# A two-block transformer kernel: rotary halves copied on ScalarE, retention values centred over each head as they leave PSUM, boundary norms split in two

## The chip, the cores and the metric

The kernel runs on one core of one Trainium2 chip. The time is that of one whole launch in microseconds (us) on the device. PE is TensorE, DVE is VectorE, ACT is ScalarE, POOL is GpSimd and SP is SyncE, which here issues every DMA.

## What is computed

Two blocks run one after the other on 256 tokens of width 1024, all in f32. The first block has two layers. A layer of it is:

```
h = rmsnorm(x, g_mix)
q_r, k_r, v_r, g_r, q_s, k_s, v_s, gate_a, gate_b = split(h @ w_in)
q_r, k_r = rotary(q_r), rotary(k_r) * 128 ** -0.5       # 4 heads of 128
ret = retention(q_r, k_r, v_r)                          # 4 heads, values of 256
ret = head_group_norm(ret) * silu(g_r)                  # (y - mean) * rsqrt(var + eps) over the 256
sb  = stick_breaking(q_s, k_s, v_s)                     # 8 heads of 128
merged = sigmoid(gate_a) * (ret @ p_ret) + sigmoid(gate_b) * (sb @ p_sb)
x = x + merged @ w_out
x = x + square(relu(rmsnorm(x, g_mlp) @ w_up)) @ w_down
```

`rotary(t)` is `[t1 * cos - t2 * sin, t1 * sin + t2 * cos]` over the two halves of a head's 128 columns. `head_group_norm` subtracts the mean of a head's 256 outputs and divides by their spread. For each token and head, retention is a weighted sum over earlier tokens of the value rows, so subtracting from every value row its own mean over the 256 columns of the head gives the same output as subtracting the mean afterwards. The second block is one layer with another mixer and the same kind of MLP, and a norm ends the whole.

## The kernel before, in words

The weights come as 201 pieces of 1 MB through a ring of four buffers (`raw`): the mixer of a layer of the first block has 44 pieces (k = 0 to 43), its MLP has 32; the second block has 17 and 32. PE works to nearly f32 precision with products of rounded parts: ACT rounds each piece to `w_hi` (L887), DVE subtracts to get `w_lo` (L1302, two instructions a piece), and PE multiplies hi by hi, hi by lo and lo by hi (all through `mm`, L488). `convert(piece)` stands for this step on either engine, and is called three pieces ahead of PE. Everything has a fixed order written out by hand on each engine, with semaphores between them; an engine that waits holds all that is behind it.

A use of a piece fills one of two pairs of PSUM banks. When PE is through with it, ACT copies one half (`carry`, L893), DVE adds the other (L1314) and frees the pair (`pair_free`), for which PE waits two uses later. Gate pieces (k = 20 to 31) have three more ACT and two more DVE instructions each.

The order of the mixer's pieces is: sbv 0 to 3, sbq/sbk 4 to 11, rq 12, 13, rk 14, 15, rv 16 to 19 (the retention values), rg 20 to 23, ga 24 to 27, gb 28 to 31, psb 32 to 35, pret 36 to 39, wout 40 to 43. `stages(k)` names small steps that each engine does at the end of piece k. Those that the change touches:

- `rotate` at k = 18 for q and at k = 19 for k. PE multiplies by the matrix `turn` (four records of 128x512), DVE multiplies the result by sin (L1464) into `ry`, POOL multiplies the original by cos (L1269), DVE adds (L1468). Then `rope_done` rises; PE waits for it at `ret_scores` of head 0, k = 21.
- `ret_out` of head h at k = 23 + 2h: PE makes the output, ACT copies it to `ry` (L980), POOL adds its halves to `rsum` (L1260).
- `ret_mean` at k = 25 + 2h: PE multiplies `rsum` by a matrix of 1/256, DVE subtracts this mean (L1475), ACT squares (L984), POOL adds (L1264, `rsq`).
- `ret_var` at k = 27 + 2h: PE takes the mean of `rsq`, ACT makes the reciprocal root (L988, L990), DVE multiplies by it (L1479), by the gate (L1482), and splits (L1484, L1308) to `retT`, which is needed at k = 36.
- Values: ACT copies one PSUM bank of rv (L1005), DVE the other (L1499), at k = 17 and 19.

Norms at the start of a layer, of the second block and at the end (`norm_rows`, `wide_rows`): ACT squares with a running sum (L899), POOL makes the factor (L1203, L1206), DVE makes `htok = xs * rstd * gain` in one instruction for each half of a tile (L1325, L1581; there are two tiles of 128 tokens). PE transposes `htok` (L520), ACT and DVE split it to `hT`. At the very start POOL raises `x_ready` for both tiles before it makes any factor, so it waits for the second tile of x. In an MLP the first use of a piece goes through `up`: DVE sums, squares, converts piece + 3 and only then rounds and splits `uT`, for which PE waits.

Of the kernel before, what the change touches and what calls it, by code (L numbers as in the profile page):

```python
# [21 lines left out]
F32 = mybir.dt.float32  # L22
# [4 lines left out]
ACT = mybir.ActivationFunctionType  # L27

# [53 lines left out]
def constants():  # L82
# [5 lines left out]
    rope = np.stack([np.cos(ang), np.sin(ang)], 1).astype(f)  # L88
# [11 lines left out]
    turn = np.zeros((P, P), f)  # L100
    turn[np.arange(half) + half, np.arange(half)] = -1.0
    turn[np.arange(half), np.arange(half) + half] = 1.0
    square = np.stack([np.eye(P, dtype=f), np.full((P, P), 1.0 / T, f), later, np.ones((P, P), f), turn], 1)
# [11 lines left out]
def build(nc, x, w_in, p_ret, p_sb, w_out, w_up, w_down, g_mix, g_mlp, g_final, norm_mix_g_2, w_in_2, pool_w_2,  # L115
# [3 lines left out]
    with ctx:  # L119
# [39 lines left out]
        sq_r = place("sq_r", [P, 5, P], F32R, at[0])  # L159
        sq_c = place("sq_c", [P, 5, P], F32)  # L160
        ident, mean_w, turn = (sq_c[:, i, :] for i in (0, 1, 4))
# [34 lines left out]
        rsum = place("rsum", [P, T], F32, htok_at)  # L196
# [4 lines left out]
        us = place("us", [P, 2, T], F32, y_at)  # L201
        usq = place("usq", [P, 2, T], F32, y_at + 2 * T * 4)
# [33 lines left out]
        def sem(name):  # L236
# [14 lines left out]
        x_ready = sem("x_ready")  # L251
# [18 lines left out]
        ret_scores, ret_decayed, ret_out, ret_copied, ret_mean, ret_centred, ret_squared, ret_var = (  # L270
            sem(n) for n in ("ret_scores", "ret_decayed", "ret_out", "ret_copied", "ret_mean", "ret_centred",
                             "ret_squared", "ret_var"))
# [53 lines left out]
        def stages(k):  # L326
# [49 lines left out]
        def _(sp):  # L376
# [42 lines left out]
            for L in range(DEPTH):  # L419
                for k in range(MIX_PIECES):  # L420
# [16 lines left out]
                    if k == 3 and L == 0:  # L437
                        sp.dma_start(sq_c[:, 1:5, :], square[:, 1:5]).then_inc(masks_in, 16)
                        sp.dma_start(mask_c[:, :], mask).then_inc(masks_in, 16)
# [38 lines left out]
            for t in range(TILES):  # L478

                sp.wait_ge(h_ready, 8 + 4 * 6 + 2 * (t + 1))  # L480
                sp.dma_start(ot[t], htok[:, t, :]).then_inc(out_sent, 16)
            sp.wait_ge(out_sent, 16 * TILES)
# [3 lines left out]
        def _(pe):  # L486
# [60 lines left out]
            def across_by_token(n, piece, use, between):  # L547
# [5 lines left out]
                hi_products(piece + 1, use + 1, 0)  # L553
                pe.wait_ge(h_lo, turned_at + 4)
# [20 lines left out]
            def mlp(n, stage, piece, use):  # L575

                turn_tile(n, 1, 0)
                across_by_token(n, piece, use, lambda: turn_tile(n, 1, 1))
# [53 lines left out]
            for L in range(DEPTH):  # L632
# [4 lines left out]
                def stage(name, i):  # L637
# [34 lines left out]
                    elif name == "rotate":  # L672

                        pe.wait_ge(pair_free, use_of("rk", 1, L).count(3))
                        pe.wait_ge(z_masked, Place(3, (L, 4)).count(1))
                        pe.wait_ge(consts_in, 32)
                        if i:
                            pe.wait_ge(rope_sin, Place(0, (L, 2)).count(1))
# [12 lines left out]

# [6 lines left out]
                    elif name == "ret_mean":  # L698
# [3 lines left out]
                        pe.wait_ge(ret_summed, head.count(0) * 2 + 1)  # L702
                        mm(ps[:, 6, 0:T], mean_w, rsum[:, :], True, True).then_inc(ret_mean, 1)
                    elif name == "ret_var":
                        pe.wait_ge(ret_summed, head.count(1) * 2)
                        mm(ps[:, 7, 0:T], mean_w, rsq[:, 0, :], True, True).then_inc(ret_var, 1)
# [68 lines left out]
            across_by_token(Place(4), Place(first), Place(use0), turn_other)  # L775
# [105 lines left out]
        def _(act):  # L881
# [13 lines left out]
            def square_sum(n, t, c):  # L895
# [3 lines left out]
                act.activation(htok[:, t, half], xs[:, t, half], ACT.Square, scale=D ** -0.5,  # L899
# [41 lines left out]
            for L in range(DEPTH):  # L941
# [3 lines left out]
                square_sum(mixer_norm, 0, 0)  # L945
                square_sum(mixer_norm, 0, 1)
                if not L:
                    convert(here)
                turned_hi(mixer_norm, 0, 0)
                turned_hi(mixer_norm, 0, 1)  # L950
                square_sum(mixer_norm, 1, 0)
                square_sum(mixer_norm, 1, 1)
# [6 lines left out]
                def stage(name, i):  # L959
# [12 lines left out]
                    elif name == "sb_out":  # L972
                        act.wait_ge(sb_out, pair.count(1))
                        act.activation(sbT[:, 2 * i:2 * i + 2, 0:T],
                                       ps[:, 6, :].rearrange("p (j t) -> p j t", j=2), ACT.Copy).then_inc(sb_hi, 1)
                    elif name == "ret_out":
                        act.wait_ge(ret_out, head.count(1))
                        if i >= 2:
                            act.wait_ge(ret_lo, head.count(-1))
                        act.activation(ry[:, i % 2, :, :], ps[:, 5, :].rearrange("p (e t) -> p e t", e=2),  # L980
                                       ACT.Copy).then_inc(ret_copied, 1)
                    elif name == "ret_mean":
                        act.wait_ge(ret_centred, head.count(1))
                        act.activation(rsq[:, :, :], ry[:, i % 2, :, :], ACT.Square).then_inc(ret_squared, 1)  # L984
# [881 lines left out]
```

## Time and profile before

| | us |
|---|---|
| median of 3 runs | 1282.72 |
| lowest, highest | 1282.07, 1284.2 |
| the profiled execution, whole | 1279.49 |
| its span, first to last instruction | 1277.7 |
| PE busy, of the span | 1233.7 |
| DVE busy | 872.8 |
| ACT busy | 629.5 |
| POOL busy | 55.0 |
| mean granted clock of TensorE | 0.999 |

The span is cut into what an engine did and what it waited for. A matmul's time in the trace overlaps with the next one's, so the cost of a matmul is read from the starts of the neighbours, not from its duration.

### The profile page before, as it was taken

Reading aid. Unit: us, or ns where it says so; the run is one execution under the profiler, and the core shown is the slowest. Engines: PE = TensorE matmul, PEld = TensorE weight load, DVE = VectorE, ACT = ScalarE, POOL = GpSimd, SP = SyncE. Lnnn points to the kernel's source line nnn. Section 1 sums busy time; section 2 is a strip of 40 time slices with the busy share of each in tenths; the row PEclk is TensorE's granted clock in tenths of the full one; section 3 lists DMA queues with packets and bytes.
Section 4 is the critical chain, followed back from the end, with each engine's and each line's share of the span. In section 5 each row is a group of like instructions: output and inputs, shape, how many; then the busy total and the mean of one; then the engine's idle time right before and its main releaser. Section 6 shows DMA issues by size and latency. Waiting matters only on the chain.

```text
span 1277.7 us, 17080 instructions
## 1 busy us (share of the span) xinstructions
PE 1233.7 (97%) x6842; PEld 1064.7 (83%) x6842; DVE 872.8 (68%) x1024; ACT 629.5 (49%) x827; POOL 55.0 (4%) x78
## 2 busy tenths in 40 slices
PE   4999999999999999999999999999989999999997
PEld 3888888788888887888888788888879997888886
DVE  4577767797566666667767887666677756766664
ACT  4455476644334434555576544443358456443442
POOL 0000110001000000000310001000010000100000
PEclk9999999999999999999999999999999999999999
DMA  5854455455555556655554555555656333555652
GB/s 199 273 159 160 138 165 159 158 176 187 171 197 182 183 194 199 191 148 161 152 162 151 164 174 188 193 179 186 213 165 190 100 100 132 185 182 192 197 181 98
DMA packets 162794, 219.92 MB, mean 172 GB/s; under 512 B 5680, under 2 KB 134064, under 8 KB 162736
## 3 DMA queue, kind: packets, MB, share of 16 engines
q1 hardware_dynamic: 162736, 219.11, 53.4%
q8 instruction: 41, 0.67, 0.2%
q14 instruction: 17, 0.14, 0.0%
HBM read 218.05 MB, written 1.05 MB: 171 GB/s over the span
## 4 chain that ended last, share of the span: by engine, by line
PE 83%; DVE 9%; ACT 4%; DMA 2%; issue 1%; POOL 0%; SPq 0%; DVEq 0%; POOLq 0%; ACTq 0%
PE ps L488 82%; DVE w_lo L1302 3%; DMA raw<-in_w_in_dram 1%; PE ps L520 1%; DMA xs<-in_x_dram 1%; ACT w_hi L887 1%; ACT carry L893 1%; DVE gates L1314 1%; ACT gates L1020 0%; DVE gtmp L1552 0%; DMA raw<-in_w_down_dram 0%; DVE gtmp L1547 0%; DVE ry L1479 0%; DVE ry L1482 0%; DVE retT L1308 0%
## 5 line engine op out<-in xcount | busy, mean ns | idle before, releaser
L488 PE MATMUL ps<-hT,w_hi 128*128 128x512 f32 (+1 forms) x1952 | 587.7, 367 | 1.6 <-DVE hT L1308 1.6
L1302 DVE TENSOR_TENSOR w_lo<-raw,w_hi 128x1024 fp32r<-128x1024 f32 x402 | 477.6, 1231 | 103.1 <-ACT w_hi L887 102.6
L887 ACT ACTIVATE w_hi<-raw 128x1024 fp32r<-128x1024 f32 x402 | 402.2, 1051 | 192.9 <-DMA raw<-in_w_up_dram 129.6
L488 PE MATMUL ps<-hT,w_lo 128*128 128x256 f32 x1696 | 455.3, 280 | 0.0
L488 PEld LDWEIGHTS ps<-hT,w_hi 128*128 128x128 f32 x1952 | 341.3, 189 | 64.1 <-DVE hT L1308 1.8
L488 PEld LDWEIGHTS ps<-hT,w_lo 128*128 128x128 f32 x1696 | 312.1, 189 | 2.4 <-issue 0.5
L488 PE MATMUL ps<-w_hi,uT 128*128 128x512 f32 x768 | 248.9, 396 | 5.0 <-DVE uT L1308 4.9
L893 ACT ACTIVATE carry<-ps 128x512 f32<-128x512 f32 x114 | 67.9, 595 | 254.8 <-PE ps L488 254.8
L488 PEld LDWEIGHTS ps<-w_hi,uT 128*128 128x128 f32 x768 | 144.3, 188 | 40.9 <-DVE uT L1308 6.4
L488 PE MATMUL ps<-w_lo,uT 128*128 128x512 f32 x384 | 151.8, 395 | 0.0
L488 PE MATMUL ps<-w_hi,hT 128*128 128x512 f32 (+1 forms) x480 | 143.5, 377 | 2.9 <-DVE hT L1308 1.5
L1374 DVE TENSOR_TENSOR us<-ps,carry 128x512 f32<-128x512 f32 x48 | 33.2, 691 | 116.2 <-ACT carry L893 116.1
L488 PEld LDWEIGHTS ps<-w_hi,hT 128*128 128x128 f32 x480 | 88.4, 190 | 19.6 <-issue 4.2
L488 PE MATMUL ps<-w_lo,hT 128*128 128x512 f32 (+1 forms) x240 | 89.1, 371 | 0.0
L488 PEld LDWEIGHTS ps<-w_lo,uT 128*128 128x128 f32 x384 | 72.2, 188 | 15.3
L488 PEld LDWEIGHTS ps<-w_lo,hT 128*128 128x128 f32 x240 | 45.7, 190 | 7.7 <-issue 0.5
L488 PE MATMUL ps<-sbT,w_hi 128*128 128x512 f32 x128 | 45.9, 400 | 0.0
L488 PE MATMUL ps<-retT,w_hi 128*128 128x512 f32 x128 | 45.3, 396 | 0.0
L488 PE MATMUL ps<-sbT,w_lo 128*128 128x256 f32 x128 | 36.1, 282 | 0.0
L488 PE MATMUL ps<-retT,w_lo 128*128 128x256 f32 x128 | 36.1, 282 | 0.0
L1378 DVE SCALAR_TENSOR_TENSOR usq<-us 128x512 f32<-128x512 f32 x48 | 33.3, 693 | 1.6
L1308 DVE TENSOR_TENSOR uT<-usq,uT 128x512 fp32r<-128x512 f32 x48 | 33.2, 693 | 1.6
(188 smaller groups left out, 946.9 us busy)
## 6 DMA issues: line engine op xcount, KB each, us to landing
raw<-in_w_in_dram SPq DMA_DIRECT2D x77, 1024.0 KB, 5.7
raw<-in_w_up_dram SPq DMA_DIRECT2D x48, 1024.0 KB, 5.4
raw<-in_w_down_dram SPq DMA_DIRECT2D x48, 1024.0 KB, 4.9
raw<-in_w_out_dram SPq DMA_DIRECT2D x12, 1024.0 KB, 5.1
raw<-in_p_sb_dram SPq DMA_DIRECT2D x8, 1024.0 KB, 5.1
raw<-in_p_ret_dram SPq DMA_DIRECT2D x8, 1024.0 KB, 5.0
xs<-in_x_dram SPq DMA_DIRECT2D x2, 512.0 KB, 6.9
gain<-in_g_mix_dram SPq DMA_DIRECT2D x2, 512.0 KB, 6.8
```

The lines of the kernel that those rows point to most:

```text
L488: return pe.matmul(o, lhsT, rhs, start=start, stop=stop)
L520: last = pe.transpose(ps[:, token_bank(t, c), k * P:(k + 1) * P], htok[:, t, c * HALF + k * P:c * HALF + (k + 1) * P], ident)
L887: act.activation(w_hi[:, s, half], raw[:, s, half], ACT.Copy).then_inc(hi_ready, 1)
L893: act.activation(carry[:, use.slot(2), :, :], ps[:, b:b + 2, T:2 * T], ACT.Copy).then_inc(pair_act, 1)
L1302: last = dve.tensor_tensor(w_lo[:, s, half], raw[:, s, half], w_hi[:, s, half].bitcast(F32), ALU.subtract)
L1308: return dve.tensor_tensor(o, value, hi.bitcast(F32), ALU.subtract)
L1314: dve.tensor_tensor(o, ps[:, b:b + 2, 0:T], carry[:, use.slot(2), :, :], ALU.add).then_inc(pair_free, 1)
L1374: dve.tensor_tensor(us[:, :, :], ps[:, b:b + 2, 0:T], carry[:, use.slot(2), :, :], ALU.add).then_inc(pair_free, 1)
L1378: dve.scalar_tensor_tensor(out=usq[:, :, :], in0=us[:, :, :], scalar=0.0, in1=us[:, :, :], op0=ALU.max, op1=ALU.mult).then_inc(u_squared, 1)
```

## The change

- Rotary: ACT copies the two halves of the partitions crosswise from `retqkv` into `ry` (two instructions of 64 partitions x 1024); the sign is in the sin table. DVE multiplies `ry` by sin in place, in SBUF. The matrix `turn` and its products are gone.
- Retention values: ACT copies nothing. DVE sums each head's 256 columns in PSUM (one reduction over both banks) and writes both banks centred (two instructions). `ret_mean`, `rsum`, the subtraction and ACT's copy of the outputs are gone. ACT squares the outputs straight from PSUM; DVE multiplies them by the gate as they leave PSUM; `ret_var` comes two pieces earlier (k = 25 + 2h). PE's `ret_out` of a head now waits until ACT and DVE have read the one before.
- Norms: DVE multiplies by the gain (`gained`) before the factor is there, and a `tensor_scalar` in place after it. The squares go to `junk` and not to `htok`.
- Start: POOL raises `x_ready` for tile 0, makes its factor, and then waits for tile 1. ACT and DVE split tile 0 before they convert piece 0.
- MLP: the first `up` rounds and splits before DVE converts piece + 3.
- Second block: PE does the first products of piece 1 before it transposes tile 1.
- End: the result leaves in four DMAs of half a tile instead of two of a tile.

```diff
                     elif name == "rotate":
-                        for j in range(2):
-                            last = mm(ps[:, 4 + j, :], turn, retqkv[:, 2 * j:2 * j + 2, i, :], True, True)
-                        last.then_inc(turned, 1)
+                        act.wait_ge(pair_free, use_of("rk", 1, L).count(3))
+                        act.wait_ge(rest_split, Place(3, (L, SB_H // 2)).count(1))
+                        if i:
+                            act.wait_ge(rope_done, Place(0, (L, 2)).count(1))
+                        swapped = ry[:, :, :, :].rearrange("p a e t -> p (a e) t")
+                        act.activation(swapped[0:P // 2], retqkv[P // 2:P, :, i, :], ACT.Copy)
+                        act.activation(swapped[P // 2:P], retqkv[0:P // 2, :, i, :], ACT.Copy).then_inc(turned, 1)
...
-                        dve.tensor_tensor(tmp, ps[:, 4:6, :].rearrange("p b (h t) -> p (b h) t", h=2),
-                                          rope_c[:, 1:2, :].to_broadcast([P, RET_H, T]), ALU.mult).then_inc(rope_sin, 1)
+                        dve.tensor_tensor(tmp, tmp, rope_c[:, 1:2, :].to_broadcast([P, RET_H, T]), ALU.mult).then_inc(rope_sin, 1)
...
-                                dve.tensor_copy(retqkv[:, 2 * (i // 2):2 * (i // 2) + 2, 3, :],
-                                                b.rearrange("p (h c) -> p h c", h=2)).then_inc(pair_free, 1)
+                                b = ps[:, bank:bank + 2, :].rearrange("p t (h c) -> p t h c", h=2)
+                                sums = v_sums[:, :].rearrange("p (t h) -> p t h", t=TILES)
+                                dve.tensor_reduce(sums, b, X_AXIS, ALU.add).then_inc(v_summed, 1)
+                                dve.wait_ge(v_summed, Place(i // 2, (L, 2)).count(1))
+                                for t in range(TILES):
+                                    last = dve.scalar_tensor_tensor(
+                                        out=retqkv[:, 2 * (i // 2):2 * (i // 2) + 2, 2 + t, :],
+                                        in0=sums[:, t, :].unsqueeze(2).to_broadcast([P, 2, T]), scalar=-1.0 / T,
+                                        in1=b[:, t], op0=ALU.mult, op1=ALU.add)
+                                last.then_inc(pair_free, 1)
...
-                        act.activation(ry[:, i % 2, :, :], ps[:, 5, :].rearrange("p (e t) -> p e t", e=2),
-                                       ACT.Copy).then_inc(ret_copied, 1)
-                    elif name == "ret_mean":
-                        act.wait_ge(ret_centred, head.count(1))
-                        act.activation(rsq[:, :, :], ry[:, i % 2, :, :], ACT.Square).then_inc(ret_squared, 1)
+                        act.activation(rsq[:, :, :], ps[:, 5, :].rearrange("p (e t) -> p e t", e=2),
+                                       ACT.Square).then_inc(ret_squared, 1)
...
                     elif name == "ret_out":
                         pe.wait_ge(ret_decayed, head.count(1))
+                        pe.wait_ge(ret_gated, head.count(0))
+                        pe.wait_ge(ret_squared, head.count(0))
...
-            for name, at_piece in (("ret_var", 27), ("ret_mean", 25), ("ret_out", 23), ("ret_scores", 21)):
+            for name, at_piece in (("ret_var", 25), ("ret_out", 23), ("ret_scores", 21)):
...
-                    dve.scalar_tensor_tensor(out=htok[:, t, q], in0=xs[:, t, q], scalar=rstd[:, t:t + 1],
-                                             in1=gain[:, n.slot(2), q], op0=ALU.mult, op1=ALU.mult).then_inc(h_ready, 1)
+                    dve.wait_ge(row_gained, m.count(0) * 4 + (2 * t + c + 1))
+                    dve.tensor_scalar(htok[:, t, q], htok[:, t, q], rstd[:, t:t + 1], None, ALU.mult).then_inc(h_ready, 1)
...
-                up(piece, use, count(0), 0, before=False)
+                up(piece, use, count(0), 0, before=False, ahead=False)
+                convert(piece + 3)
...
-            across_by_token(Place(4), Place(first), Place(use0), turn_other)
+            across_by_token(Place(4), Place(first), Place(use0), lambda: None, turn_other)
```

## Rows read from the trace of the kernel before

**Rows 1.** The page, part 1: busy time, share, count

```profile
PE 1233.7 (97%) x6842; PEld 1064.7 (83%) x6842; DVE 872.8 (68%) x1024; ACT 629.5 (49%) x827; POOL 55.0 (4%) x78
```

**Rows 2.** Waits of PE: waiting, releaser, total us, times, longest

```profile
...
PE ps L488 <- POOL rsq L1264: 5.2, 2, 2.6
PE ps L488 <- DVE uT L1308: 4.9, 3, 1.6
...
PE ps L520 <- DVE htok L1581: 2.0, 1, 2.0
```

**Rows 3.** Timeline of PE, first layer: start, length, what

```profile
143.03 1.93 PE L488 MATMUL ps<-retqkv,sq_c 128*128 128x512 f32 x4
...
144.40 0.79 PE L488 MATMUL ps<-w_hi,hT 128*128 128x512 f32 x1
...
145.03 0.39 PE L488 MATMUL ps<-w_lo,hT 128*128 128x512 f32 x1
...
189.32 0.59 PE L488 MATMUL ps<-rsum,sq_c 128*128 128x256 f32 x2
...
189.75 1.47 PE L488 MATMUL ps<-rs,retqkv 128*128 128x256 f32 x8
```

**Rows 4.** Timeline ahead of the variance product of head 3, first layer

```profile
243.14 0.68 DVE L1475 TENSOR_TENSOR ry<-ry,ps 128x512 f32<-128x512 f32 x1
243.86 0.63 ACT L984 ACTIVATE rsq<-ry 128x512 f32<-128x512 f32 x1 [3.27 <-DVE ry L1475]
...
244.56 0.73 POOL L1264 TENSOR_TENSOR rsq<-rsq 128x256 f32<-128x256 f32 x1 [14.15 <-ACT rsq L984]
```

**Rows 5.** Timeline of DVE at the start of the first MLP

```profile
313.38 2.35 DVE L1302 TENSOR_TENSOR w_lo<-raw,w_hi 128x1024 fp32r<-128x1024 f32 x2
...
316.11 0.69 DVE L1308 TENSOR_TENSOR uT<-usq,uT 128x512 fp32r<-128x512 f32 x1
```

**Rows 6.** The start: one DMA with its landing, then the timeline

```profile
gain<-in_g_mix_dram SPq DMA_DIRECT2D x1, 512.0 KB, 5.4
...
1.48 0.34 SPq L387 DMA_DIRECT2D gain<-in_g_mix_dram  x1
...
4.42 0.63 ACT L899 ACTIVATE htok<-xs 128x512 f32<-128x512 f32 x1 [2.40 <-POOLq L1231]
...
11.73 2.00 ACT L887 ACTIVATE w_hi<-raw 128x1024 fp32r<-128x1024 f32 x2 [5.98 <-DMA raw<-in_w_in_dram]
...
14.25 1.42 DVE L1325 SCALAR_TENSOR_TENSOR htok<-xs,rstd,gain 128x512 f32<-128x512 f32 x2 [14.25 <-POOL rstd L1206]
...
18.64 0.77 PE L488 MATMUL ps<-w_hi,hT 128*128 128x512 f32 x1 [1.55 <-DVE hT L1308]
```

**Rows 7.** Timeline around the rotary steps, first layer

```profile
145.04 2.42 POOL L1269 TENSOR_TENSOR retqkv<-retqkv,rope_c 128x1024 f32<-128x1024 f32 x1 [125.05 <-PE ps L488]
...
145.13 0.85 ACT L971 ACTIVATE wts<-logw 128x768 f32<-128x768 f32 x1 [2.35 <-DVE logw L1452]
...
152.06 4.57 DVE L1302 TENSOR_TENSOR w_lo<-raw,w_hi 128x1024 fp32r<-128x1024 f32 x2 [0.25 <-ACT w_hi L887]
...
152.25 3.30 POOL L1269 TENSOR_TENSOR retqkv<-retqkv,rope_c 128x1024 f32<-128x1024 f32 x1 [4.79 <-PE ps L488]
...
164.51 0.70 PE L488 MATMUL ps<-retqkv 128*128 128x256 f32 x3
```

**Rows 8.** Groups by line: shapes, count, busy us, mean ns, idle before

```profile
L887 ACT ACTIVATE w_hi<-raw 128x1024 fp32r<-128x1024 f32 x402 | 402.2, 1051 | 192.9 <-DMA raw<-in_w_up_dram 129.6 <-DMA raw<-in_w_in_dram 41.0 <-DMA raw<-in_w_down_dram 16.5
...
L1547 DVE TENSOR_SCALAR gtmp<-gates 128x512 f32<-128x512 f32 x16 | 6.8, 427 | 0.5
...
L1468 DVE TENSOR_TENSOR retqkv<-retqkv,ry 128x1024 f32<-128x1024 f32 x4 | 4.9, 1226 | 2.5 <-POOL retqkv L1269 2.3
L1464 DVE TENSOR_TENSOR ry<-ps,rope_c 128x1024 f32<-128x1024 f32 x4 | 4.9, 1214 | 0.0
```

**Rows 9.** Timeline at the end

```profile
1273.25 1.41 DVE L1325 SCALAR_TENSOR_TENSOR htok<-xs,rstd,gain 128x512 f32<-128x512 f32 x2 [1.83 <-POOL rstd L1206]
```

More of the change, by code:

```diff
@@ L87, in constants @@
     ang = np.arange(T, dtype=f)[None, :] * np.concatenate([inv_freq, inv_freq])[:, None]
-    rope = np.stack([np.cos(ang), np.sin(ang)], 1).astype(f)
+    turned_sign = np.where(np.arange(P) < half, f(-1.0), f(1.0))[:, None]
+    rope = np.stack([np.cos(ang), np.sin(ang) * turned_sign], 1).astype(f)
     s, t = np.arange(P)[:, None], np.arange(P)[None, :]
@@ L99, in constants @@
     later = (s > t).astype(f)
[L100 to L103, printed above, removed]
+    square = np.stack([np.eye(P, dtype=f), np.full((P, P), 1.0 / T, f), later, np.ones((P, P), f)], 1)
     levels = np.zeros((P, MASKED, CHUNK), f)
@@ L158, in build @@
         gn_eps = place("gn_eps", [P, 1], F32)
-        sq_r = place("sq_r", [P, 5, P], F32R, at[0])
-        sq_c = place("sq_c", [P, 5, P], F32)
-        ident, mean_w, turn = (sq_c[:, i, :] for i in (0, 1, 4))
+        v_sums = place("v_sums", [P, 2 * TILES], F32)
+        sq_r = place("sq_r", [P, 4, P], F32R, at[0])
+        sq_c = place("sq_c", [P, 4, P], F32)
+        ident, mean_w = (sq_c[:, i, :] for i in (0, 1))
         later, ones = sq_r[:, 2, :], sq_r[:, 3, :]
@@ L478, in _ @@
             for t in range(TILES):
-                sp.wait_ge(h_ready, 8 + 4 * 6 + 2 * (t + 1))
-                sp.dma_start(ot[t], htok[:, t, :]).then_inc(out_sent, 16)
-            sp.wait_ge(out_sent, 16 * TILES)
+                for c in range(2):
+                    half = slice(c * HALF, (c + 1) * HALF)
+                    sp.wait_ge(h_ready, 8 + 4 * 6 + 2 * t + c + 1)
+                    sp.dma_start(ot[t][:, half], htok[:, t, half]).then_inc(out_sent, 16)
+            sp.wait_ge(out_sent, 16 * 2 * TILES)
         @block.tensor
@@ L545, in lo_products, with across_by_token @@
                 last.then_inc(piece_used, 1)
-            def across_by_token(n, piece, use, between):
+            def across_by_token(n, piece, use, between, after):
                 turned_at = n.count(0) * 4
@@ L553, in across_by_token @@
                 hi_products(piece + 1, use + 1, 0)
+                after()
                 pe.wait_ge(h_lo, turned_at + 4)
@@ L697, in stage @@
                         last.then_inc(ret_out, 1)
-                    elif name == "ret_mean":
+                    elif name == "ret_var":
                         if i == 0:
                             pe.wait_ge(sb_lo, Place(3, (L, 4)).count(1))
[L702 to L705, printed above, removed]
+                        pe.wait_ge(ret_summed, head.count(1))
                         mm(ps[:, 7, 0:T], mean_w, rsq[:, 0, :], True, True).then_inc(ret_var, 1)
@@ L1405, in _, with row @@
                 before = (Place(1), Place(1), Place(0), Place(MIX_PIECES))
+                def row(t, c):
+                    if L:
+                        down_sum(*before, t, c)
+                    gained(mixer_norm, mixer_norm, Place(L), t, c)
+                row(0, 0)
+                row(0, 1)
                 if L:
-                    down_sum(*before, 0, 0)
-                    down_sum(*before, 0, 1)
                     convert(here + 1)
-                norm_rows(mixer_norm, Place(L), 0)
+                norm_rows(Place(L), 0)
                 if L:
-                    down_sum(*before, 1, 0)
-                else:
-                    convert(here)
+                    row(1, 0)
                 turned_lo(mixer_norm, 0, 0)
                 turned_lo(mixer_norm, 0, 1)
-                if L:
-                    down_sum(*before, 1, 1)
-                norm_rows(mixer_norm, Place(L), 1)
+                if not L:
+                    convert(here)
+                    row(1, 0)
+                row(1, 1)
+                norm_rows(Place(L), 1)
                 if not L:
```

125 lines of the change are left out of this document (62 added, 63 removed).

## The prediction

> **What bounds the kernel now.** I read the page's busy times first. PE is busy 1233.7 us of a span of 1277.7, 97% [rows 1]; DVE, next, has 68%. So work taken from PE counts in full, idle time of PE counts in full, and time of DVE, ACT or POOL counts only where PE ends up waiting for it. The second view is what PE waited for. Three entries of it are places that the change touches: 5.2 us in two waits for POOL's `rsq`, 4.9 us in three waits for `uT`, and 2.0 us for `htok` at the second block's start [rows 2]. The wait before the first transpose is the start of the program and is read from its timeline. Third, I read the timeline of each place, since a step's worth is that of the wait that ends last there. The granted clock is at full rate over nearly all of the span, so no stretch but the start is priced at the half rate.
>
> **Rotary products.** Four `rotate` steps (two a layer) leave PE. One starts at 143.03, the next ordinary product at 144.40, and that product's record is 0.79 long where its neighbour's is 0.39 [rows 3]: 1.37 + 0.40 = 1.77 us each, so 4 x 1.77 = 7.1 us off PE.
>
> **Mean products.** From the start of the `rsum` product to the next one are 189.75 - 189.32 = 0.43 us [rows 3]. Eight of them: 3.4 us.
>
> **The wait for the variance.** In each layer PE stands 2.6 us before the last `ret_var`. What comes late is a chain through DVE's subtraction, ACT's square and POOL's sum, 243.14 to 245.3 [rows 4], and DVE reaches that subtraction late since it runs behind PE through the gate pieces. After the change the square reads PSUM directly, at ACT's step of k = 29, with no DVE instruction ahead of it in the chain, and PE asks for the sum at the end of k = 31. PE's 1233.7 us over 201 pieces are 6.1 us each with the small steps, some 5.6 without; by two gate pieces of that length there are about 4 us of room. I take the wait as gone: 2 x 2.6 = 5.2 us. Bounds 0 and 5.2: if DVE lags so far that ACT's gate steps slip, part stays.
>
> **The MLP's first product.** PE waits 1.6 us, three times, for `uT` [rows 2]. Ahead of its rounding DVE does a conversion of 2.35 us [rows 5]. With this moved behind, `uT` comes 2.3 us earlier, which is more than 1.6: 4.9 us gained. What is late next is the moved conversion itself. It would end about 1.2 us later than now, but PE first does a down product of some 5.6 us, so it is covered; were that cover gone, it would cost 1.2 each.
>
> **The start.** Now the first product starts at 18.64 [rows 6]. The chain to it goes through the factor, which POOL makes only when the second tile of x is in; the rows of `htok` start at 14.25. After the change, tile 0 is squared from 4.42, the factor is there at about 6.8, and the gain lands at 1.48 + 5.4 = 6.9. Two gain multiplications (0.69 each), two scalings (0.43) and the transposes and splits end by 12.3. Then the weights are last: ACT rounds piece 0 from 11.73 to 13.73 and DVE's two conversions follow it half by half, to 15.15. So the first product starts near 15.2: 3.4 us earlier. Piece 1 must be ready 4.7 us on; its rounding waits for its landing and DVE's conversion comes after the gain and the rows of tile 1. I get 19.8 against a need of 19.9, where before PE stood 0.4: 3.9 us in all. Products at this point run at half the later pace, as their starts show; if the clock rises not with the products but at the same instant as now, up to 1.7 us of the gain is lost. Bounds 2 and 4.5.
>
> **Second block's start.** PE now idles 2.0 us for tile 1's `htok` [rows 2] with 1.9 us of products still in hand. The change does these first, but then PE stands until ACT and DVE have split tile 1, about 2 us after the transpose. The rows of tile 1 themselves come 0.3 us sooner, through the shorter instruction. Net 0.9 us; bounds 0 and 2.0.
>
> **The end.** After the last factor DVE needs 1.41 us [rows 9]; with two `tensor_scalar` at 0.43 [rows 8] it needs 0.86, 0.55 less. The last DMA carries half, and starts while the first half is on its way: some 0.6 less. 1.2 us; bounds 0.5 and 1.6. The 0.43 is measured with a constant, and the new instruction takes its scalar per partition, which no row here shows for this operation. The Trainium skill (VectorE: DVE Perf Modes, The perf-mode tier table) puts f32 `tensor_scalar` from SBUF at twice the rate of `tensor_tensor`, with no exception for such a scalar; if it did not hold, the end would gain about 0.6 and not 1.2.
>
> Sum of gains: 7.1 + 3.4 + 5.2 + 4.9 + 3.9 + 0.9 + 1.2 = 26.6 us. At a layer's start in the second layer PE waits for the split, which doesn't move: nothing.
>
> **What the change adds: the rotary stretch.** This is where PE's products are replaced by work of engines that are less busy, but in a chain with a date: `rope_done` must be up when PE ends piece 21. I follow the first layer on its own time axis. ACT ends the weights' exponential at 145.13 + 0.85 = 145.98 [rows 7]; then come its two copies. No row shows 64 partitions from one half to the other; the nearest is 1.05 for 128x1024 [rows 8], which I take; below it could be nothing less than half, above it twice if crossing partitions costs. So `turned` is up at 148.1 (before: 145.0). Now DVE multiplies by sin, 1.23 from SBUF for the sum of the same shape [rows 8], and POOL by cos, 2.42 alone. Do they run side by side? Before, DVE read PSUM there, and lost nothing. But at 152.06, when DVE's two conversions with both inputs in SBUF fell on POOL's second cos, they took 4.57 and not 2.35, and POOL took 3.30 and not 2.42 [rows 5, 7]: DVE lost 2.2. So I put the two in series: 148.1 + 1.23 + 2.42, and DVE's sum of 1.23: 153.0. Then ACT copies for k, 155.1. DVE meanwhile does the values of k = 19: the reduction of 1024 elements from PSUM at 1.21 for the nearest row [rows 8], two centrings at 0.69: 155.8. POOL's second cos runs to 157.6 and holds DVE's conversion of piece 22, which ends at 160.0; sin 161.2; sum 162.5. PE ended piece 21 at 164.51 [rows 7]; less the two rotary steps of 3.5 it is there at 161.0. It stands 1.4 us. DVE then is behind PE by a piece and frees PSUM pairs late: about 0.7 us more until k = 24 (its step of a gate piece, 4.1 plus two turns of 0.6 with ACT, is just under PE's 5.6, so it hardly catches up, but falls no further). 2.1 us a layer, 4.2 in all. Bounds 0 (copies of half the length) and 10 (copies of double length, 4.2 more on the chain).
>
> The Trainium skill (SBUF — State Buffer, Who interferes with whom) calls this an exclusive lock: a DVE instruction with two SBUF inputs and a GpSimd one that reads SBUF exclude each other for a whole instruction. The rows agree: 3.30 is 2.42 and most of a conversion, 4.57 is 2.35 and most of the cos. It speaks against moving the sin product to SBUF; without such a lock the chain would be 1.2 us shorter.
>
> **What hides the rest.** The values at k = 17: 2.6 us on DVE for 0.69 before; DVE has idle time before its next conversion, and the pair is wanted two uses on. Gate multiplication moves from `ret_var` to `ret_out`: DVE now waits at k = 23 for ACT's square (0.6), but saves the subtraction (0.68) for each head. ACT no longer waits for `ret_lo` or the centring in the middle of its queue, which had held its next `carry`. PE's new waits at `ret_out` (`ret_gated` of the head before, a DVE step of two pieces earlier): by the same count DVE is through 2 to 4 us before PE asks. These go at 0, bounds -1 and 2 us in all.
>
> **Sum.** 26.6 - 4.2 = 22.4 us. The span goes from 1277.7 to 1255.3, the profiled execution from 1279.49 to 1257.1. The median of the runs lies 3.2 us above that execution, so the forecast is 1282.72 - 22.4 = 1260.3.
>
> **Rivals.**
> *The rotary stretch is covered.* ACT copies of half the partitions are cheap, or DVE's order absorbs them. For it: DVE is busy 68% of the span, and its idle time lies in just such places. Then 1282.7 - 26.6 = 1256.1. Chance 0.22.
> *DVE's lag spreads.* For it: DVE runs only a few tenths per piece faster than PE through the gates, so a lag of a piece lasts; against: it is never two pieces. With 5 us a layer: 1282.7 - 26.6 + 10 = 1266.1. Chance 0.15.
> *Slower than before.* The crosswise copy is the one unmeasured operation on a dated chain. It stands four times, two instructions each. If `rope_done` came over 13.3 us after PE wants it in each layer (copies of 4 us or so each instead of 1.05), the gain would be used up; at 5 us each the four copies of a layer add 4 x 3.95 = 15.8 to the chain, 2 x (15.8 + 2.1) - 26.6 = 9.2 lost: 1291.9. Against: every ACT copy in the trace goes by elements per partition. Chance 0.03.
> *The boundaries don't give what they say.* The conversion moved behind `uT`, the early factor and the split rows only shift which wait is last; half of 4.9 + 3.9 + 0.9 + 1.2 stays: 1265.8. Chance 0.07.
> The forecast as worked out has 0.53.
>
> **Numbers.** Range 1254.5 to 1267. A measurement of this kernel tells about 0.2% (2.6 us) from no change. Faster by more: 0.96; within: 0.01; slower: 0.03.
>
> **What would show it.** PE's busy time down by about 10 us, no records of `turn` or `rsum`; no wait for `rsq`, none for `uT`; the first product near 15.2; a new wait of PE for `retqkv` (L1468's sum) of 1 to 1.5 us, twice; crosswise copies near 1.05 us. The forecast is wrong if the copies take twice that, if PE shows waits for `pair_free` through the gate pieces, or if the first product starts after 17.

## The result

The changed kernel takes 1264.74 us (median of 4 runs, 1264.06 to 1265.52) against 1282.39 for the kernel before in the same series: a ratio of 0.9874, 95% interval 0.9859 to 0.989. The forecast was 1260.3, with a range of 1254.5 to 1267. The sign and most of the gain were right, and the time lies in the range, 4.4 us above the forecast. One run of the kernel with the old addresses (below) took 3145 us and is left out; the median of its other five is 1261.33, where the expectations have 1261.84. The profiled execution of after took 1264.06 us with a span of 1262.2, where before it was 1279.49 and 1277.7. The busy line and PE's waits in the profile of after (waiting, releaser, total us, times, longest):

```profile
PE 1230.4 (97%) x6810; PEld 1062.0 (84%) x6810; DVE 882.0 (70%) x1040; ACT 630.2 (50%) x823; POOL 53.3 (4%) x70
```

```profile
PE ps L489 <- DVE w_lo L1292: 4.6, 2, 4.1
PE ps L489 <- DVE hT L1298: 3.1, 2, 1.6
...
PE ps L489 <- DVE retqkv L1469: 2.1, 2, 1.1
PE ps L489 <- DVE gtmp L1304: 1.4, 2, 1.1
...
PE ps L521 <- DVE htok L1596: 0.6, 1, 0.6
```

Against [rows 2] the waits for `rsq` and for `uT` are gone, `htok` fell from 2.0 to 0.6, and the new wait for `retqkv` (the rotary sum, L1469) is there, twice. All of that was forecast. Two things don't fit. L1304 is the sum with which DVE frees a PSUM pair; PE waits for it at k = 34 of both layers, 0.3 and 1.1 us. The forecast had pairs freed late only up to k = 24, at 0.7 us a layer. And PE's busy time fell by 3.3 us against [rows 1], where the products taken out are worth 10.5. So PE does the work that is left more slowly, and no wait shows this.

The start, in the timeline of after:

```profile
7.31 0.87 DVE L1322 TENSOR_SCALAR htok<-htok,rstd 128x512 f32<-128x512 f32 x2
...
10.40 1.99 ACT L877 ACTIVATE w_hi<-raw 128x1024 fp32r<-128x1024 f32 x2
...
11.48 2.36 DVE L1292 TENSOR_TENSOR w_lo<-raw,w_hi 128x1024 fp32r<-128x1024 f32 x2 [0.25 <-ACT w_hi L877]
...
13.99 0.76 PE L489 MATMUL ps<-w_hi,hT 128*128 128x512 f32 x1 [4.12 <-DVE w_lo L1292]
```

The rows of the first tile are made at 7.31 where [rows 6] have 14.25, and then the weights are last, as forecast. The first product starts at 13.99, not 15.2: piece 0 could be rounded at 10.40, where [rows 6] have 11.73.

The rotary stretch of the first layer in after:

```profile
141.53 1.06 ACT L975 ACTIVATE ry<-retqkv 64x1024 f32<-64x1024 f32 x1
...
142.60 1.06 ACT L976 ACTIVATE ry<-retqkv 64x1024 f32<-64x1024 f32 x1
...
143.69 1.23 DVE L1466 TENSOR_TENSOR ry<-ry,rope_c 128x1024 f32<-128x1024 f32 x1 [3.06 <-ACT ry L976]
143.73 3.47 POOL L1259 TENSOR_TENSOR retqkv<-retqkv,rope_c 128x1024 f32<-128x1024 f32 x1 [128.27 <-ACT ry L976]
...
147.24 1.23 DVE L1469 TENSOR_TENSOR retqkv<-retqkv,ry 128x1024 f32<-128x1024 f32 x1 [2.32 <-POOL retqkv L1259]
...
150.78 2.45 POOL L1259 TENSOR_TENSOR retqkv<-retqkv,rope_c 128x1024 f32<-128x1024 f32 x1 [3.58 <-ACT ry L976]
150.83 4.61 DVE L1292 TENSOR_TENSOR w_lo<-raw,w_hi 128x1024 fp32r<-128x1024 f32 x2
...
156.68 1.23 DVE L1469 TENSOR_TENSOR retqkv<-retqkv,ry 128x1024 f32<-128x1024 f32 x1
...
157.96 0.92 PE L489 MATMUL ps<-retqkv 128*128 128x256 f32 x4 [1.01 <-DVE retqkv L1469]
```

The copies take 1.06 each (forecast 1.05). POOL's product, 2.42 alone [rows 7], takes 3.47 beside DVE's sine product of 1.23, which is near the sum of the two, 3.65. DVE's conversion takes 4.61 beside the other, which is close to 2.35 + 2.45. PE then waits 1.01, forecast 1.4.

### The profile page after: what moved, and what is told of

It is laid out like the page before. It is cut to its first block, busy times and chain, and to the rows that moved or that the text cites. A ratio compares the mean times of both kernels' runs of the same rounds, so it can differ in the third digit from the quotient of the medians.

```text
span 1262.2 us, 17060 instructions
## 1 busy us (share of the span) xinstructions
PE 1230.4 (97%) x6810; PEld 1062.0 (84%) x6810; DVE 882.0 (70%) x1040; ACT 630.2 (50%) x823; POOL 53.3 (4%) x70
## 3 DMA queue, kind: packets, MB, share of 16 engines
HBM read 217.98 MB, written 1.05 MB: 174 GB/s over the span
## 4 chain that ended last, share of the span: by engine, by line
PE 59%; issue 19%; DVE 13%; ACT 5%; DMA 2%; POOL 2%; DVEq 0%; SPq 0%; POOLq 0%; ACTq 0%
PE ps L489 59%; DVE w_lo L1292 5%; DVE gtmp L1561 1%; DMA raw<-in_w_in_dram 1%; DVE gates L1304 1%; DVE gtmp L1556 1%; ACT gates L1015 1%; DMA decay_c<-in_decay_dram 1%; ACT w_hi L877 1%; PE ps L521 1%; POOL retqkv L1259 1%; POOL gr L1246 1%; DVE retT L1484 0%; ACT junk L891 0%; DVE ry L1482 0%
```

## Experiments

Times below are medians beside runs of the kernel before on the same chip (1280.86, 1280.84 and 1281.82 us in the three series). Where single stages are compared, I take the same instruction in two traces (ACT's `carry` number n) and look how far one kernel is ahead. The old-address kernel, the early copies and the conversion put back ran in different series; the kernel before differs by 1 us between these.

**The two kernels again.**

> The kernel before, unchanged, beside the changed kernel on one chip. In the two profiles, four pieces of an MLP took 22.31 us before and 22.46 us after, 0.7% more, though the loop is the same. Theory A, the pace belongs to the chip or the execution: here before and after show the same MLP pace, within 0.1%, and the span of before is near 1282 to 1284 if the pace is the slow one. Theory B, the change makes PE slower: before keeps 22.31 and after 22.46 side by side.

> The changed kernel, unchanged. Theory A: the same MLP pace as the kernel before on this chip, and 17 to 20 us less than it at that pace. Theory B: 22.46 us for four pieces against 22.31. In both, two stretches of half clock of 3.4 us, one at the second block's start and one at its wout products, if they belong to the kernel; at other places or missing if they are chance.

Before: 1280.22 us, a single run. After: 1264.68 (1263.25 to 1266.19), ratio 0.9883, 0.9867 to 0.99. The medians of the two series differ by 16.2 and 17.7 us. The paces are those of the first two traces, 22.31 and 22.47, so Theory B holds. Of the stretches at half clock the one at the second block's start came again, at 942.9; the other did not, and the kernel before had one of its own at 245.4.

**The order of the second block's start, undone.**

```diff
-            across_by_token(Place(4), Place(first), Place(use0), lambda: None, turn_other)
+            across_by_token(Place(4), Place(first), Place(use0), turn_other, lambda: None)
```

> Changed kernel with the second block's tile 1 transposed between the hi products of pieces 0 and 1 again, as before. Theory A, that the new order puts PE's idle time of the second block's start together (1.6, 0.6, 0.9 and 1.55 us within 10 us) and that the clock falls for it: the half clock there is gone and the kernel is 1 to 2 us faster than the changed one. Theory B, that the half clock comes by chance of position: it stays, and this order is 0 to 1 us slower.

1265.37 us, 0.9877 (0.9858 to 0.9897): no difference from after beyond the noise of some 2 us. PE's wait for `htok` is back (2.5 us against 0.6), and a wait for `hT` is gone (1.6 against 3.1). One wait is exchanged for the other: the term is worth nothing that can be measured. The half clock at the second block's start is gone, as Theory A said, but the trace has a stretch of 6.8 us at 974.1 instead, in a wait of 2.9 us for `hq`, so the time doesn't fall.

**PE's rotary products back in the changed kernel.** The matrix `turn`, its products and the sine product from PSUM are as before; the rest of the change stays.

> Changed kernel with the rotary products on PE again (the matrix, DVE's product from PSUM), all else as changed. The prediction's step: the swap takes 1.77 us off PE four times and gives 2.1 a layer back as waits, so this kernel is 2.9 us slower than the changed one, about 1267.5; its PE has no wait for retqkv L1469. The rival that the rotary stretch costs nothing: 7 us slower. That it costs more than it gives: faster than the changed one. Its tiles lie 32 bytes further than before, so its pace tells on the address theory too: A says 22.46, B leaves it open.

1265.62 us, 0.9881 (0.9859 to 0.9903): the same as after within the noise, and less than the 1267.5 expected. Its MLP pace is that of after, as theory A of the addresses said. PE has no wait for `retqkv`, and the four `turn` steps instead. By the traces the mixers of the two layers are 1.0 and 0.3 us slower than with the copies: the swap is worth 1.3 us, where the forecast had 7.1 - 4.2 = 2.9.

**The rotary steps two pieces earlier.**

```diff
-            if k in (18, 19):
-                todo.append(("rotate", k - 18))
+            if k in (16, 17):
+                todo.append(("rotate", k - 16))
...
-                        act.wait_ge(rest_split, Place(3, (L, SB_H // 2)).count(1))
```

> Changed kernel with the rotary steps two pieces earlier (k = 16 and 17), without the wait for rest_split. Theory A, that the rotary chain is late by 1 to 2 us a layer for PE: PE's waits for retqkv L1469 and the late pair_free go, 2 to 4.5 us faster than the changed kernel. Theory B, that DVE's total work in the stretch is what counts and not the date of the chain: the wait only moves to another line, 0 to 1 us.

1276.47 us, 0.9963 (0.9949 to 0.9977), 11.8 slower than after. Neither theory had this. Its waits of PE begin:

```profile
PE ps L489 <- DVE rest_lo L1297: 14.9, 3, 6.3
```

The steps now stand on ACT and DVE ahead of the last stick-breaking split, for which PE has a date too. The waits for `retqkv` and for the pair are gone. From inside the two waits of 6.3 us come stretches at half clock of 10.2 and 6.8 us, which are part of the loss. In the first layer a DVE instruction of 0.95 fell on POOL's product and took 3.09:

```profile
135.09 2.39 POOL L1258 TENSOR_TENSOR retqkv<-retqkv,rope_c 128x1024 f32<-128x1024 f32 x1 [117.99 <-ACT ry L975]
135.21 3.09 DVE L1447 SCALAR_TENSOR_TENSOR zs<-zs,soft 128x768 f32<-128x768 f32 x1
```

**PE's pace: addresses or instructions?** The rows below are ACT's `carry` behind one up-projection of the first MLP and behind the one 20 pieces on, where PE never waits: first before, then after. The rows of after stand one up-projection later in the MLP; the pace is even over both stretches.

```profile
328.31 0.60 ACT L893 ACTIVATE carry<-ps 128x512 f32<-128x512 f32 x1 [5.42 <-PE ps L488]
...
439.84 0.60 ACT L893 ACTIVATE carry<-ps 128x512 f32<-128x512 f32 x1 [3.52 <-PE ps L488]
```

```profile
327.28 0.60 ACT L883 ACTIVATE carry<-ps 128x512 f32<-128x512 f32 x1 [3.61 <-PE ps L489]
...
439.64 0.60 ACT L883 ACTIVATE carry<-ps 128x512 f32<-128x512 f32 x1 [3.69 <-PE ps L489]
```

Twenty pieces take 111.53 us before and 112.36 after, 0.7% more, with the same products at the full clock. The change takes out one matrix of 512 bytes per partition and puts in sums of 32 bytes, so the tiles behind them lie 480 bytes lower, an odd multiple of 32. The weights and `hT` lie ahead of them and did not move; `uT` did. Four kernels ask what makes the difference. The first gives the changed kernel the old addresses:

```diff
-        v_sums = place("v_sums", [P, 2 * TILES], F32)
...
+        v_sums = place("v_sums", [P, 2 * TILES], F32)
+        place("unused", [P, 120], F32)
```

> Changed kernel with every tile behind sq_c at its address in the kernel before (the change moved them by -480 bytes, an odd multiple of 32), by 480 unused bytes. Nothing else differs. Side by side on one chip the MLP went at 22.31 us for four pieces before and at 22.45 to 22.47 after. Theory A, the pace comes from where the tiles lie: 22.31 here, and a kernel 5 to 8 us faster than the changed one, 1257 to 1260. Theory B, it comes from the order and number of PE's instructions: 22.45 to 22.47 and 1264 to 1265 here.

1261.33 us, 0.9846 (0.9825 to 0.9866): by the medians 3.4 us faster than after, less than the 5 to 8 expected. In the profiles PE is busy 4.0 us less (1226.4 for 1230.4), with the same 6.8 us at half clock in each.

```profile
328.05 0.60 ACT L884 ACTIVATE carry<-ps 128x512 f32<-128x512 f32 x1 [3.49 <-PE ps L490]
...
439.58 0.60 ACT L884 ACTIVATE carry<-ps 128x512 f32<-128x512 f32 x1 [3.67 <-PE ps L490]
```

111.53 us, the pace of before, with the instructions of after. The second moves the tiles of the kernel before by 32 bytes (`place("unused", [P, 8], F32)` ahead of them):

> The kernel before with 32 unused bytes ahead of sq_r, so that all later tiles lie 32 bytes further. Theory A (addresses): the MLP pace goes from 22.31 to about 22.46 and the kernel is 4 to 8 us slower than before. Theory B (instructions): no change, within 1 us.

1288.21 us, 1.0058 (1.0037 to 1.0079), at the pace of after: 112.36. Not all of the 7.4 us is pace, since its trace has three stretches of 3.4 us at half clock where the first trace of before has none ahead of the end. The third only adds an instruction to PE's queue (`pe.wait_ge(small_set, 1)`, ahead of the layers):

> Changed kernel with one more instruction on PE, a wait for something long since there, ahead of the first layer. Theory B, that the place of PE's instructions in memory sets the pace: another pace than 22.45 to 22.47 in some of the MLPs. Theory A: the same pace.

1264.34 us, a single run, with the pace of after unchanged. With the first kernel, where the pace changed and the instructions did not, this leaves the place of PE's instructions without support as a cause. A fourth, in the kernel before, lowers one tile alone:

```diff
-        uT = place("uT", [P, 3, 2, 2 * T], F32R, u_at)
+        uT = place("uT", [P, 3, 2, 2 * T], F32R, u_at - 32)
```

> The kernel before, with one tile alone 32 bytes lower: the MLP's activation uT, which its down-projections stream. If the pace follows the address of the tile that streams, four pieces take between 22.31 and 22.46 us: the half of the products that stream uT are slow and those that stream hT keep their pace, so about 22.38, and 1.5 to 2 us on the whole. If it follows the address of the matrix that is loaded (the pieces' high and low parts, which do not move here), 22.31 and no difference. If any odd multiple of 32 does it to all, 22.46 and about 3.6 us.

1284.31 us, 1.0021 (1.0011 to 1.0032).

```profile
330.41 0.60 ACT L893 ACTIVATE carry<-ps 128x512 f32<-128x512 f32 x1 [5.55 <-PE ps L488]
...
442.44 0.60 ACT L893 ACTIVATE carry<-ps 128x512 f32<-128x512 f32 x1 [3.68 <-PE ps L488]
```

112.03 us: 0.50 of the 0.83. So one tile alone makes 60% of the loss; which other tile gives the rest was not tried. The expectation has two things wrong, though. In `mm(out, loaded, streamed)` a down-projection passes `uT` as the matrix that is loaded and streams the weights (`three`); `hT` is streamed by the up-projections (`across`), with the weights loaded. And the time is not lost where `uT` is read. In the trace's names the streamed tile stands first. Each series below is the first product of one up-projection, of the down-projection behind it, and of the next up-projection: before, then with `uT` moved.

```profile
322.56 0.39 PE L488 MATMUL ps<-hT,w_hi 128*128 128x512 f32 x1
...
328.11 0.39 PE L488 MATMUL ps<-w_hi,uT 128*128 128x512 f32 x1
...
333.71 0.39 PE L488 MATMUL ps<-hT,w_hi 128*128 128x512 f32 x1
```

```profile
324.56 0.39 PE L488 MATMUL ps<-hT,w_hi 128*128 128x512 f32 x1
...
330.21 0.40 PE L488 MATMUL ps<-w_hi,uT 128*128 128x512 f32 x1
...
335.82 0.40 PE L488 MATMUL ps<-hT,w_hi 128*128 128x512 f32 x1
```

The up-projection takes 5.55 and 5.65 us, the down-projection 5.60 and 5.61. From here on, with `uT` moved, every second up-projection takes 5.65 and the others 5.55. Over ten of each, the up-projections take 55.54 us before, 55.99 with `uT` moved and 56.20 in after; the down-projections 55.99, 56.05 and 56.17. So most of the loss lies in products that read neither `uT` nor any other tile that moved. The runs show that the layout sets the pace; they don't show by what way, and PE's own reads of the moved tile can't be all of it. Nor does a run show that odd multiples of 32 are what matters: every shift tried (480, 32 and 32 bytes the other way) was one, and no even multiple was tried.

**The MLP's first conversion back ahead of `uT`** (from here on with the old addresses, so beside 1261.33):

```diff
-                up(piece, use, count(0), 0, before=False, ahead=False)
-                convert(piece + 3)
+                up(piece, use, count(0), 0, before=False)
```

> The changed kernel with the tiles at the old addresses (1261.84 us), but the first up-projection converts piece + 3 ahead of the rounding of its own activation, as before the change. Theory of the prediction (the reorder is worth 1.6 us three times, 4.9 us; the trace after gave 1.9 three times): three waits for uT of 1.6 us are back and the time is 1266.5 to 1267.5 us. Rival (the conversion only moves, so the next products wait for it anyway): no more than 2 us slower, under 1264 us, with a wait for the converted piece gone in exchange.

1266.46 us, 0.9878 (0.9862 to 0.9893): 5.1 slower by the medians and 4.1 by the ratios, as the theory said, and the line is back:

```profile
PE ps L490 <- DVE uT L1299: 4.9, 3, 1.6
```

**Copies and cosine product one piece earlier, DVE's part where it was.**

```diff
+            if k in (17, 18):
+                todo.append(("turn_in", k - 17))
...
-                    elif name == "rotate":
+                    elif name == "turn_in":
 
                         act.wait_ge(pair_free, use_of("rk", 1, L).count(3))
-                        act.wait_ge(rest_split, Place(3, (L, SB_H // 2)).count(1))
...
-                        elif name == "rotate":
+                        elif name == "turn_in":
```

> The changed kernel with the tiles at the old addresses (1261.84 us), and of the rotary swap only ScalarE's two copies and GpSimd's cosine product go ahead by one piece, into the hole of ScalarE beside the last 2.3 us for the decay rows; VectorE's sine product and sum keep their place. Theory (the chain copy, product, sum sets a date that TensorE waits for): TensorE's two waits for the turned values (2.2 us in all) and half of the 2 us of late work behind them go, 1258 to 1260 us, and no row of waits names L1470. Rival (what costs is VectorE's work itself and the port that it shares with GpSimd): the conversion of 1.2 us that now lies beside the cosine product stretches as the other did (4.6 us), the first waits for decay or pieces return, and the time is 1261 to 1266 us. A copy of 1.06 us needs no longer while a piece is converted.

1255.93 us (1254.78 to 1257.63), 0.9794 (0.978 to 0.9807): 5.4 us faster by the medians than the same kernel without this edit, and 5.4 in the traces at the end of the second layer's MLP. It is the fastest kernel here that does all the work. The gain is larger than the 2 to 4 expected. No wait names the rotary sum. Its timeline:

```profile
135.41 1.06 ACT L977 ACTIVATE ry<-retqkv 64x1024 f32<-64x1024 f32 x1
...
136.48 1.06 ACT L978 ACTIVATE ry<-retqkv 64x1024 f32<-64x1024 f32 x1
...
137.62 2.84 POOL L1261 TENSOR_TENSOR retqkv<-retqkv,rope_c 128x1024 f32<-128x1024 f32 x1 [120.89 <-ACT ry L978]
...
138.66 4.01 DVE L1294 TENSOR_TENSOR w_lo<-raw,w_hi 128x1024 fp32r<-128x1024 f32 x2 [0.48 <-ACT w_hi L880]
...
154.18 1.23 DVE L1471 TENSOR_TENSOR retqkv<-retqkv,ry 128x1024 f32<-128x1024 f32 x1
...
157.86 0.82 PE L492 MATMUL ps<-retqkv 128*128 128x256 f32 x4
```

DVE's conversions are still stretched (4.01 here for 2.35), but the second sum ends 2.5 us before PE wants it. To see what that gives, take ACT's `carry` at k = 14 and k = 34 of the first layer, the latter in the `p_sb` product: before, old addresses, and this kernel.

```profile
114.65 0.60 ACT L893 ACTIVATE carry<-ps 128x512 f32<-128x512 f32 x1 [2.97 <-PE ps L488]
...
251.83 0.60 ACT L893 ACTIVATE carry<-ps 128x512 f32<-128x512 f32 x1 [1.78 <-PE ps L488]
```

```profile
110.80 0.60 ACT L884 ACTIVATE carry<-ps 128x512 f32<-128x512 f32 x1 [2.97 <-PE ps L490]
...
242.35 0.60 ACT L884 ACTIVATE carry<-ps 128x512 f32<-128x512 f32 x1 [3.55 <-PE ps L490]
```

```profile
111.29 0.60 ACT L886 ACTIVATE carry<-ps 128x512 f32<-128x512 f32 x1 [3.16 <-PE ps L492]
...
240.71 0.60 ACT L886 ACTIVATE carry<-ps 128x512 f32<-128x512 f32 x1 [3.09 <-PE ps L492]
```

137.18, 131.55 and 129.42 us. The forecast's gains for one layer, without any cost of the rotary stretch, are 2 x 1.77 + 4 x 0.43 + 2.6 = 7.9; the first and third differ by 7.76. In the second layer the three are 137.19, 132.34 and 129.31, so 7.88. The sum of the gains is thus confirmed, not each of them.

**Without POOL's cosine product.** Its two instructions a layer are left out, so the rotary values are not the reference's:

```diff
-                            pool.tensor_tensor(v, v, rope_c[:, 0:1, :].to_broadcast([P, RET_H, T]),
-                                               ALU.mult).then_inc(rope_cos, 1)
+                            pool.sem_inc(rope_cos, 1)
```

> The changed kernel with the tiles at the old addresses (1261.84 us), without GpSimd's cosine product (its two instructions per layer are left out, so the rotary values are wrong; nothing else is). It gives the price of what lies beside it: theory (the port is what makes VectorE late: its conversion took 4.6 us beside the product of 2.45 us and GpSimd's other product 3.5 us): that conversion takes 2.2 to 2.4 us, the sums come 2 to 3 us earlier, the waits for L1470 go, and the time is 1257.5 to 1260 us. Rival (VectorE has the slack, and copies and sums alone set the date): within 1 us of 1261.84.

1253.77 us, 0.9788 (0.9769 to 0.9807), faster than either side expected. DVE's conversion is at its length alone:

```profile
149.71 2.35 DVE L1292 TENSOR_TENSOR w_lo<-raw,w_hi 128x1024 fp32r<-128x1024 f32 x2
```

At the end of the second layer's MLP it is 5.9 us ahead of the same kernel with the product, and only 0.5 ahead of the kernel with early copies. So when the chain starts a piece earlier, the cosine product and what it stretches cost next to nothing. This kernel leaves out the product and the stretching together, so it doesn't part the two.

## Why the prediction was right, and where it missed

The mechanism held: the waits and products that it named are gone, and the rotary stretch costs PE something in each layer. That the time still lies in the range owes something to the width of the range, since two costs of some 3 us each were in no term.

Each term of the sum, measured between the kernel before and the changed kernel with the old addresses, which run at one pace:

- *Start*, 3.9 forecast: 4.0. Right: the first product starts at 15.09, 3.6 us earlier (forecast 3.4). In after it started at 13.99, since piece 0 could be rounded sooner there; over the traces with the new start it lies between 13.99 and 16.16, with the rounding of piece 0 between 10.40 and 12.57. The kernel before varies in the same way (17.63 to 19.05), so a pair of traces tells this term to 2 us or so.
- *Mixers of the two layers* (rotary and mean products, variance wait, less the rotary stretch), 15.7 - 4.2 = 11.5 forecast: 5.6 + 4.9 = 10.5. The early copies show the sum of the gains to be right, 7.76 and 7.88 of 7.9. The term that was mis-sized is the stretch: 2.2 and 3.0 us instead of 2.1 each. The working had the mechanism, down to the length of the conversion. PE's wait for the sum was 1.1 us in each layer and not 1.4; its waits for a free pair, forecast at 0.7 up to k = 24, were 0.2 and 0.9, nearly all at k = 34; the remaining 1 us a layer is in no large wait of the profile, and it goes with the wait when the copies come earlier. So the 0.7 for all that DVE's lag costs behind the sum was too little.
- *MLP's first product*, 4.9 forecast: 5.8 by the traces (1.9 three times), 4 to 5 by the runs with it undone. Right, within 1 us.
- *Second block's start*, 0.9 forecast: 0.3 lost by the traces, no difference by the run with it undone. PE stands 0.62 us for `htok` where it stood 1.96, but then 1.55 us for the split of that tile, during which, before, it had products to do. The step that failed is the balance of the two: the 1.9 us of products moved ahead do not shorten the way through transpose and split, and this way costs PE all that they hide.
- *End*, 1.2 forecast: about 0.8, within its bounds. The last factor's rows take less, as the rule on `tensor_scalar` had it (the Trainium skill, VectorE: DVE Perf Modes, The perf-mode tier table), also with a scalar per partition:

```profile
1258.62 0.88 DVE L1322 TENSOR_SCALAR htok<-htok,rstd 128x512 f32<-128x512 f32 x2 [1.10 <-POOL rstd L1204]
```

That is 0.88 where [rows 9] have 1.41.

Two things were in no term. The first is the addresses: 3.4 us by the medians, 3.6 by the traces. With the half clock (below), which adds some 3.2 us to PE's busy time in after, they account for a fall of 3.3 us instead of 10.5. I read "PE's busy time falls by 10 us" from records taken out, and took for granted that the records left keep their length. The diff shows two tile declarations changed; I passed over them.

The second is the clock. The forecast took full rate from the profile of before for every stretch but the start. The profile of after has two stretches of half rate (granted clock 0.5, 1.2 GHz), 3.4 us each, at 942.0 and 1051.2; the first began in a wait of PE of 1.6 us, the second 1.3 us behind one of 2.6. The columns are stretch, length, PE busy, granted clock, DMA share, GB/s:

```profile
1051.20:1054.60 3.40, 3.40 (x10) 0.50 0.15 57
1055.00:1058.00 3.00, 3.00 (x14) 1.00 0.00 0
```

The same sixteen products of the second block take 3.51 us in after and 2.18 with the old addresses, where they ran at full rate:

```profile
942.36 3.51 PE L489 MATMUL ps<-hT,w_hi 128*128 128x256 f32 x16 [1.55 <-DVE hT L1298]
```

```profile
940.96 2.18 PE L490 MATMUL ps<-hT,w_hi 128*128 128x256 f32 x16 [1.55 <-DVE hT L1299]
```

Both stood 1.55 us before, so the wait alone doesn't decide it. The kernel with the old addresses has its stretch at 971.1 instead, 6.8 us long, from inside a wait of 3.1 for `hq` that lasts 1.2 us more. The second execution of the kernel before has one of 3.4 at 245.4, behind the variance wait, where the first has none. A stretch of 3.4 us in which PE doesn't stand does 1.7 us less work.

The account for the kernel with the old addresses: 22.4 forecast, less 1.6 for the misses of the terms (+0.1, -1.0, +0.9, -1.2, -0.4), less 2.8 for the clock (half of the 5.6 us in which PE did not stand) is 18.0; the spans differ by 17.1. Of the 0.9 between, 0.5 lies in the second block behind its start, where PE waits 3.1 us for `hq` and before waited 1.7; the rest is not assigned. For after: 22.4 less 1.6, less some 3.6 for the addresses, less 3.2 for the clock is 14.0, and the spans differ by 15.5. Of the 1.5 between, 0.7 is the start of this execution. The rest fits the wait for `hq`, which is 1.3 us here instead of 3.1: PE comes there later for the half clock, and so part of that loss is taken back.

Of the rivals, the one with slow copies fell with the first row of 1.06. *The boundaries don't give what they say* had 1265.8, the nearest to the time, but not by its reason: of the 10.9 us of these terms 10.3 stayed in the traces. *DVE's lag spreads* had 1266.1: there is a wait for a free PSUM pair, but of 1.1 us at most, and the stretch cost 5.2 us in all and not 10. *The stretch is covered* describes what the kernel with early copies then does: 1255.93, where that rival said 1256.1. That the two agree so closely is partly chance, since this kernel too has the loss at the second block and one half-rate stretch, which that rival had not.

## What to carry to other kernels

When work moves from the full engine to engines with room, look at the date of the chain first: moving only its head by one piece, into an idle hole, with the busy engine's steps left in place, brought 5.4 us where the whole swap had brought 1.3; moving all of it by two pieces brought a loss of 11.8 us. No run moved all of it by one piece. After any change in what is allocated, compare the pace of a stretch without waits in both traces before explaining the sum; a product that is 0.7% slower shows in no wait. And check in the code which operand is loaded and which is streamed before building a test on it. Count short stalls of PE with some loss of clock behind them as a cost in the range, since they come at different places from one execution to the next.

## What the runs showed of the hardware

- The layout of SBUF changes PE's pace at full clock: twenty pieces took 111.53 us, 112.36 with the tiles behind `sq_c` moved by 480 or by 32 bytes, and 112.03 with `uT` alone moved by 32; padding of 480 bytes restored 111.53. Of the 0.50 lost with `uT` alone, 0.45 is in up-projections, which don't read `uT`. Why is open.
- Stretches at half rate, 1.2 GHz, came in lengths of 3.4, 6.8 and 10.2 us. Those inside the program began during a wait of PE of 1.6 to 6.3 us or within 1.6 us behind one, but not at each such wait and not in each execution.
- ACT copies 64 partitions x 1024 from one half of the partitions to the other in 1.06 us, as long as 128 x 1024 without crossing [rows 8].
- DVE instructions with both inputs in SBUF and POOL's product exclude each other. Which of the two is stretched changes with who starts first: POOL with 3.47 for 2.42, DVE with 4.61 for 2.35, or DVE with 3.09 for 0.95. The Trainium skill's rule of an exclusive lock (SBUF — State Buffer, Who interferes with whom) agrees with all three rows.
